# Making the relative-position vectors of the dilated attention one product earlier

## The reference, cut to what matters

```python
u = rms_norm_2(h, mix_norm_pre[l])
proj = u @ w_in[l]
q, k, v, xr, yr, gl = jnp.split(proj, splits, axis=-1)
...
# dilated attention, three groups (window, dilation) of four heads
scores = jnp.einsum('bnqphe,bnkphe->bphnqk', qb, kb).astype(jnp.float32) * scale
bucket = t5_causal_bucket(jnp.maximum(steps, 0) * d)
bias = jnp.transpose(bias_table_g[bucket], (2, 0, 1)).astype(jnp.float32)
scores = scores + bias[None, None, :, None]
...
# recurrence: a causal convolution of xr, two gates from it, a scan
gate_x = jax.nn.sigmoid(jnp.einsum('bshi,hij->bshj', xh, w_x) + b_x).reshape(B, S, C)
gate_a = jax.nn.sigmoid(jnp.einsum('bshi,hij->bshj', xh, w_a) + b_a).reshape(B, S, C)
```

## Time and profile before

| | us |
|---|---|
| median of 3 runs | 2868.61 (2864.35 to 2872.7) |
| the profiled execution | 2872.09 |
| its span, first to last instruction | 2870.3 |
| PE busy | 2793.1 (97%) |
| DVE busy | 1451.1 (51%) |
| ACT busy | 1061.6 (37%) |

### The profile page before, as it was taken

The page is one execution under the profiler, slowest core; times in us unless marked ns, Lnnn a source line. Parts: engine busy times, 40 slices in busy tenths (PEclk is TensorE's granted clock), DMA queues, the critical chain, the costliest instruction groups (busy, mean ns, idle before and its releaser), DMA issues.

```text
span 2870.3 us, 38465 instructions
## 1 busy us (share of the span) xinstructions
PE 2793.1 (97%) x16326; PEld 2259.3 (79%) x16326; DVE 1451.1 (51%) x2394; ACT 1061.6 (37%) x1618; POOL 14.5 (1%) x30
## 2 busy tenths in 40 slices
PE   8988999999999999999999999999999999999997
PEld 6787688888887778888887888876788788888886
DVE  5834476552525666655346443274633444654433
ACT  5533453332324664433234222244333422432221
POOL 0000000000000000000000000001000000000000
PEclk9999999999999999999999999999999999999999
DMA  4200022222431002322223222236222222222221
GB/s 149 91 5 3 30 88 96 96 93 91 140 119 45 1 1 74 107 92 96 95 81 102 90 95 96 95 112 118 78 85 78 73 90 94 88 96 96 95 90 66
DMA packets 68861, 238.84 MB, mean 83 GB/s; under 512 B 7976, under 2 KB 10536, under 8 KB 68180
## 3 DMA queue, kind: packets, MB, share of 16 engines
q1 hardware_dynamic: 62064, 220.41, 22.7%
q10 hardware_dynamic: 6628, 15.98, 2.5%
HBM read 228.23 MB, written 6.03 MB: 82 GB/s over the span
## 4 chain that ended last, share of the span: by engine, by line
PE 92%; DVE 4%; ACT 3%; issue 1%; DMA 0%; ACTq 0%; SPq 0%; DVEq 0%
PE psum L153 23%; PE psum L155 23%; PE psum L154 23%; PE psum L1269 3%; PE psum L1248 2%; PE psum L1256 2%; PE psum L199 2%; PE psum L823 2%; PE psum L200 2%; PE psum L207 1%; PE psum L1790 1%; PE psum L176 1%; PE psum L175 1%; PE psum L174 1%; PE psum L1968 1%
## 5 line engine op out<-in xcount | busy, mean ns | idle before, releaser
L153 PE MATMUL psum<-x_hi,w_hi 128*128 128x512 f32 x2120 | 856.4, 404 | 0.1
L155 PE MATMUL psum<-x_hi,w_lo 128*128 128x512 f32 x2120 | 840.3, 396 | 0.0
L154 PE MATMUL psum<-x_lo,w_hi 128*128 128x512 f32 x2120 | 839.9, 396 | 0.0
L128 DVE TENSOR_TENSOR w_lo<-raw,w_hi 128x1024 fp32r<-128x1024 f32 x409 | 499.8, 1224 | 359.0 <-ACT w_hi L121 358.7
L121 ACT ACTIVATE w_hi<-raw 128x1024 fp32r<-128x1024 f32 x409 | 427.8, 1049 | 344.2 <-DMA raw<-w_down 84.6
L153 PEld LDWEIGHTS psum<-x_hi,w_hi 128*128 128x128 f32 x2120 | 399.4, 188 | 103.3 <-issue 7.1
L154 PEld LDWEIGHTS psum<-x_lo,w_hi 128*128 128x128 f32 x2120 | 399.7, 189 | 99.3 <-issue 5.3
L155 PEld LDWEIGHTS psum<-x_hi,w_lo 128*128 128x128 f32 x2120 | 399.3, 188 | 97.2
L153 PE MATMUL psum<-h_hi,w_hi 128*128 128x512 f32 x616 | 244.2, 396 | 0.0
L154 PE MATMUL psum<-h_lo,w_hi 128*128 128x512 f32 x616 | 244.2, 396 | 0.0
L155 PE MATMUL psum<-h_hi,w_lo 128*128 128x512 f32 x616 | 244.2, 396 | 0.0
(11 more groups left out here) (408 smaller groups left out, 3318.2 us busy)
## 6 DMA issues: line engine op xcount, KB each, us to landing
raw<-w_up SPq DMA_DIRECT2D x88, 512.0 KB, 3.2
raw<-w_down SPq DMA_DIRECT2D x44, 512.0 KB, 3.2
raw<-w_f1up SPq DMA_DIRECT2D x44, 512.0 KB, 3.2
raw<-w_f2up SPq DMA_DIRECT2D x44, 512.0 KB, 3.2
raw<-w_qkv SPq DMA_DIRECT2D x36, 512.0 KB, 3.3
raw<-w_blend SPq DMA_DIRECT2D x28, 512.0 KB, 3.2
raw<-w_f1down SPq DMA_DIRECT2D x22, 512.0 KB, 3.2
raw<-w_f2down SPq DMA_DIRECT2D x22, 512.0 KB, 3.2
```

The source lines that it names most:

```text
L128: dve.tensor_tensor(self.w_lo[u % SLOTS][:], self.raw[u % SLOTS][:], self.w_hi[u % SLOTS][:].bitcast(F32), ALU.subtract).then_inc(self.lo_ ...
L153: pe.matmul(bank[:], hi, x_hi[:, kk], start=kk == 0, stop=False)
L154: pe.matmul(bank[:], hi, x_lo[:, kk], start=False, stop=False)
L155: mm = pe.matmul(bank[:], lo, x_hi[:, kk], start=False, stop=kk == kt - 1)
```

## The change

The two matmuls and the two subtractions move out of `qkv0` (h = 1) into `xr`, ahead of and behind tile 5. The banks are 6 and 7 in place of 3 and 7. The loads and their order are as they were, and so are the write to HBM at h = 2 and gate 1's wait for `rel_made`.

```diff
+REL_TILE = 5
...
+    picked, made = sem("rel_picked"), sem("rel_made")
+    c, half = mem.lru_small, SKEW // 2
+    vectors = [(k.psum[0:12, 6 + j, 0:half], slice(j * half, (j + 1) * half)) for j in range(2)]
+
+    def pe(pe):
+        k.pe_head(pe, g, norm)
+        for t in range(HEADS_OUT, KD):
+            if t == REL_TILE:
+                norm.rn_ready(pe)
+                k.tile_kept(pe, g, 0)
+                pe.wait_ge(mem.loaded_rel, 48)
+                for bank, cols in vectors:
+                    mm = pe.matmul(bank, mem.table[:], mem.pick[:, cols], start=True, stop=True)
+                mm.then_inc(picked, 1)
+            k.pe_tile(pe, g, t)
...
                 dve.scalar_tensor_tensor(out=mem.xc[:, t, d:T], in0=k.sq[t % 2][:, 0:T - d], scalar=k.v(f"lconv_w{3 - d}", t),
                                          in1=mem.xc[:, t, d:T], op0=ALU.mult, op1=ALU.add).then_inc(after, 1)
+            if t == REL_TILE:
+                dve.wait_ge(picked, 1)
+                for bank, cols in vectors:
+                    dve.tensor_tensor(mem.rv[:, cols], mem.rmask[:, cols], bank, ALU.subtract).then_inc(made, 1)
...
-        if h == 1:
-            k.tile_kept(pe, self.source, 3)
-            pe.wait_ge(mem.loaded_rel, 48)
-            for j, bank in enumerate((3, 7)):
-                mm = pe.matmul(k.psum[0:12, bank, 0:SKEW // 2], mem.table[:], mem.pick[:, j * SKEW // 2:(j + 1) * SKEW // 2],
-                               start=True, stop=True)
-            mm.then_inc(self.picked, 1)
...
-        if h == 1:
-            mem, half = self.mem, SKEW // 2
-            dve.wait_ge(self.picked, 1)
-            for j, bank in enumerate((3, 7)):
-                dve.tensor_tensor(mem.rv[:, j * half:(j + 1) * half], mem.rmask[:, j * half:(j + 1) * half],
-                                  self.k.psum[0:12, bank, 0:half], ALU.subtract).then_inc(self.made, 1)
```

More of the change, by code:

```diff
@@ L1710, in lru_input @@
     first, tap1, tap2, tap3, sp = (sem(f"lru_{n}") for n in ("first", "tap1", "tap2", "tap3", "sp"))
-    c = mem.lru_small
+    picked, made = sem("rel_picked"), sem("rel_made")
[12 more added lines that the diff above has]
+            k.pe_tile(pe, g, t)
     def act(act):
@@ L1741, in dve @@
         dve.tensor_scalar(c[:, 3], c[:, 1], -4.0, None, ALU.mult).then_inc(sp, 1)
-    k.phases.append(Phase(act=act, pe=lambda pe: k.pe_normed(pe, g, norm), dve=dve))
+    k.phases.append(Phase(act=act, pe=pe, dve=dve))
     return g
@@ L1757, in __init__ @@
             sem(f"lru_{n}") for n in ("pair", "gx", "ga", "ex", "th", "own", "q", "root", "b", "h"))
-        self.picked, self.made, self.written = sem("rel_picked"), sem("rel_made"), sem("rel_written")
+        self.made, self.written = sem("rel_made"), sem("rel_written")
         self.ones = sem("dl_ones")
```

## The result

The changed kernel is slower: 2872.64 us, median of 18 runs (2868.6 to 2876.63), against 2866.02 us for 18 runs of before (2863.84 to 2872.7). The ratio is 1.0018, 95% interval 1.0012 to 1.0025, so +5.2 us (3.4 to 7.2); the two medians by themselves lie 6.6 us apart, which is within that interval. The profiled execution took 2868.6 us, span 2866.8.

A forecast was written before the change was run, and what follows sets the result against it. PE, busy 2793.1 of 2870.3 us, was taken to bound the kernel. The sum +6.45 + 1.8 - 0.35 - 3.39 - 1.8 = +2.7 us, on a median of 2868.61, gave 2871.3 us, range 2863.5 to 2877.

The forecast's parts named there:

- +6.45 (wait for the loads): At tile 5 of xr, PE stands still 6.45 us until the small loads land, behind 2 MB of gate weights.
- - 1.8 (clock after it): At gate 1, the half clock behind the old wait goes, giving back 1.8 us.
- + 1.8 (clock after it): At tile 5, half clock follows the new wait and costs 1.8 us, with bounds 0 and 3.6.
- - 3.39 (wait at gate 1): At gate 1, PE's 3.39 us wait goes because DVE does the subtractions earlier.
- - 0.35 (tile 6): At tile 6 of xr, PE's small wait for the weights' low part goes, saving about 0.35 us.
- the loads are there in time: Rival at tile 5: small loads land before PE comes, sum -5.5 us, 2863.1 us; chance 0.08.
- The same wait with another clock: Rival behind tile 5's wait: no clock price, +0.9 us, chance 0.12; or twice the price, +4.5 us, chance 0.14.
- The others: Rivals: gate 1's wait stays, +7.9 us, chance 0.05; loads land much later at tile 5, +8.6 us, chance 0.03.

The follow-up runs named there:

- e6: The two matmuls ahead of tile 7 of xr, the subtractions left in qkv0 as in the kernel before; ratio 0.9995 to before, wait at gate 1 3.39 us.
- e2: The changed kernel with the two matmuls ahead of tile 7 in place of tile 5, subtractions still behind tile 5; ratio 0.9991 to before.
- e1: The changed kernel with the three small loads issued ahead of the two 1 MB gate weights; ratio 0.9991 to before, wait at tile 5 2.23 us.
- e4: The changed kernel with the three small loads issued between the two 1 MB gate weights; ratio 1.0009 to before, wait at tile 5 3.33 us.
- e3: The changed kernel with 26 matmuls that nothing needs filling the standstill ahead of the wait for the loads; ratio 1.0007 to before.
- e10: The changed kernel run again for its trace; 46.58 us from tile 4's last matmul in xr to the second matmul behind gate 1.
- e11: A repeat of the changed kernel with the two matmuls ahead of tile 7, subtractions still behind tile 5; ratio 0.9995 to before.
- e8: The changed kernel with the vectors one tile later, matmuls ahead of tile 6 and subtractions behind its taps; ratio 0.9993 to before.
- e7: The kernel before with 13 matmuls that nothing needs filling the wait at gate 1; ratio 0.9994 to before.

## Why the prediction was right, and where its size was off

The mechanism was right at each step but one, the low clock behind the old wait. The wait at gate 1 went, because the subtractions moved ahead on DVE (e6 against e2). The matmuls were neutral in themselves (e6). The wait for the small loads took its place, because they stand behind the gates' weights on ACT's queue (e1, e4). A low clock followed it (e3). The time rose, by less than 0.3%.

The size was off, +2.7 against a measured +5.2. Two terms of the sum were mis-sized by about 1.1 us each, the wait for the loads and the clock given back at gate 1, and the clock at tile 5 by 0.7.

- "+6.45 (wait for the loads)". The traces have 7.73 us (1893.01 + 0.23 to 1900.97) and 0.35 less in e10. I took the queue's last packet for the release. In the changed kernel PE was released 0.6 us or more after q10's last packet, and the packets themselves came 6.8 to 7.2 us after PE, not 6.3 to 6.5.
- "- 1.8 (clock after it)" at gate 1. I gave this back whole. The wait of 3.39 us brings the low clock in two of five traces, so my estimate of its mean price is 0.7 us: 2/5 of 1.7, the difference between 42.5 and 40.8. Five traces leave that share rough. This was the step of the mechanism that failed, a price taken as certain. One trace of before had the low clock, and nothing in it told that the next would not.
- "+ 1.8 (clock after it)" at tile 5. The low clock lasted 5.67 and 5.43 us of PE's work, not 3.41. It cost 2.5 to 2.6 us (e3).
- "- 3.39 (wait at gate 1)". Measured 40.8 - 37.2 = 3.6. "- 0.35 (tile 6)": what went there was 0.4 us, counted from tile 5's last matmul to tile 6's second as the prediction did (0.38 in the first trace of before, 0.47 and 0.41 in e2 and e11).

With these the sum is 7.6 + 2.5 - 0.4 - 3.6 - 0.7 = +5.4 us, beside 5.2 from the times, and 46.80 - 41.98 = 4.8 from the means of the traces.

The forecast of 2871.3 is nearer to the measured median, 2872.64, than its terms were, and that is luck: it started from a median of three runs, 2868.61, while 18 runs have 2866.02, and the 2.6 us too much there nearly cancel the 2.5 us too little in the sum. Of the rivals, "the loads are there in time" didn't come about, and e1 shows that even the first place in the queue would not have been enough at tile 5. Its price was too high as well: at tile 7, where it does hold, the kernel gained 1.4 to 2.6 us (2.9 by the traces) and not 5.5, for the clock's share and for the wait for the biases that followed. "The same wait with another clock" is what happened, with a price of 2.5 us behind the new wait, between the 1.8 forecast and its double; but that rival had left the old wait's price as it was. The others were not seen.

## What to carry to other kernels

Ask of an operation that is moved ahead what it drags along: its inputs' loads were harmless at the old place and not at the new one. How late they were was decided by what stood ahead of them on their queue (waits of 7.2 to 7.6, 3.3 and 2.2 us in the changed kernel, e4 and e1). Move only the engine that is late: here the subtractions on DVE, with the matmuls held back until the loads are there (e2). Then look at what the earlier work behind it will wait for: e2 and e11 gave back 1.9 of their 4.8 us. And a price read behind one wait in one trace may be there in some executions only; before it goes into a sum, look for the same wait in another trace.

## What the runs showed of the hardware that was not expected

- The same wait of 3.4 us of PE was followed by 3.41 us at half clock in two of five executions, and by none in three. Behind waits of 1.39 and 2.23 us, with the short passes of the vectors next, there were 3.41 us of it too (e8, e1, one trace each), and behind 3.33 us 6.48 (e4). So the length of the wait alone doesn't tell the price. All fourteen traces have one more wait alike, of 2.48 or 2.49 us, in the attention near 2030: in eleven of them 3.41 us at half clock begin within 1.3 us of its end, and in e2, e3 and e8 there are none. The Trainium skill (TensorE: Matmul & The Clock Gate, Part 1) calls the number of slow matmuls at a kernel's start "run-variable"; these traces show the same of waits in the middle of a kernel.
- Loads of 112 KB, first in their queue, took 6.5 us from the end of the last issue to PE's release, while the other queue moved 2 MB (e1, one trace).
- With matmuls that nobody needs in the new standstill the clock stayed at full (e3), where both traces without them had it at half for 10.24 us. They are no gain over having no wait: e3's stretch is 6.6 us above e2's. In the kernel before (e7) they show nothing, since the clock stayed at full there without them as well, in some executions.
